# A long convolution's complex product finished on VectorE, with one inverse table and one matmul per class instead of two

## The chip, the cores and the metric

The kernel runs on one core of one Trainium2 chip. The metric is the device time of one execution in microseconds; the median of three runs counts, and lower is better.

## The reference, cut to what matters

The kernel computes one layer of a bidirectional encoder over two sequences, one of 1024 and one of 512 tokens, in fp32. Half of the mixer's width, 512 channels, goes through two gated long convolutions one after the other, each done with Fourier transforms:

```
def long_conv(z, ks, d):
    zf = jnp.fft.rfft(z, n=2 * L, axis=1)
    return jnp.fft.irfft(zf * ks[None], n=2 * L, axis=1)[:, :L] + d * z

z = x1.astype(F32) * long_conv(v.astype(F32), kspec[:, 0], bias[0])
return x2.astype(F32) * long_conv(z, kspec[:, 1], bias[1])
```

The change concerns `zf * ks`, a product of complex numbers element by element, and the first step of `irfft` behind it. The other half of the width is an mLSTM with four heads of 128 channels. Ahead of both stands an input projection, and behind them an output projection and a gated MLP.

## The kernel before

The kernel has three stages that follow one another: projections, filters and gates; then `long_convolutions_and_heads`; then the output projection and the MLP. The change lies in the second, which in the profile runs from about 766 to 1150 us.

**Tiles.** The 512 channels are worked on in two halves of HC = 256. A stream is a sequence with one half, so there are four streams: 0 and 1 for the long sequence, 2 and 3 for the short. A transform is done in two steps of matmuls. `split` (L1799) goes from tokens to classes of frequencies, and a shuffle by DMA (L1656) brings each class to its own tile. Then `forward` (L1811) transforms within a class. Two classes make a pair. The long sequence has 8 pairs and the short 4, so with two orders of convolution and two halves there are 48 pairs in all, numbered g = 0 to 47 in the order of `turns`. For each pair:

- `forward(g)` on PE: two matmuls of 128 x 128 by 128 x 256, one per class u, into `xacc[g % 2]`. Each is carried out in two passes, so the profile counts four instructions.
- `multiply(g)` on VectorE (L1983 to L1985): the spectrum in PSUM times the filter `kf` in SBUF. Partitions 0 to 63 (SUB = 64) hold real parts and 64 to 127 imaginary parts. Three products write four quarters of `prod`: real times real with imaginary times imaginary in one instruction of 128 partitions, and the two crossed products in instructions of 64 partitions, which read one half of the partitions of one operand and the other half of the other.
- `inverse(g)` on PE (L1822): for each class two matmuls, with `tab[...][1]` and `tab[...][2]`, added up in PSUM in `gacc`. They join the four quarters with their signs and transform back in one. That makes four matmuls, eight passes in the profile.
- ScalarE copies `gacc` into `classes` (L1907).

When all pairs of a stream are done, a shuffle (L1662) brings the classes back, and `join` (L1833) with `finish` on VectorE (L1993) makes tokens of them, times the gate.

**Order.** `pair_step(g)` puts `inverse(g - 2)` ahead of `forward(g)` (lag = 2). One list, `schedule`, holds the steps of convolutions and heads; the heads' steps (keys, link, attend, weight, add, square, reduce, root, unit, turn_head) are spread between them by shares written in the code. Each engine goes through the same list and carries out its part of each step, in order. In an engine's queue a step that waits holds up all behind it. `multiply(g)` stands at the place of `forward(g)`.

**Waits.** The semaphore `multiplied` counts finished products. It releases `inverse(g)`, `xacc` for `forward(g + 2)`, and the filter buffer (a ring of three) for SP's next load of `kf` (L1636). The product waits in its turn for `inverse(g - 2)` by `g_ready`, since `prod` has two buffers.

**Where lines lie.** L1883 and L1882 are the heads' attend matmuls, L1853 and L1858 keys, L1869 link and L1891 turn_head, all on PE. On VectorE L2006 weighs, L2021 to L2038 add states, L2056 to L2075 normalise heads over 512 or 1024 columns, and L2085 scales the result. L1968 is the square root on ScalarE. The inverse tables are loaded in the first stage (L841) by 12 DMAs.

## Time and profile before

| | us |
|---|---|
| median of 3 runs | 2406.47 |
| lowest, highest | 2402.73, 2407.73 |
| the profiled execution | 2401.68 |
| its span, first to last instruction | 2399.9 |
| PE busy | 2273.4 |
| VectorE busy | 1189.4 |
| ScalarE busy | 786.0 |

The profile is of one execution. Engines are called PE (TensorE matmuls), PEld (its weight loads), DVE (VectorE), ACT (ScalarE), POOL (GpSimd) and SP, the queue that issues most DMAs. PE's matmuls are pipelined, so the busy time of one overlaps that of the next, and a merged row of several tells the rate better than the duration of one. In rows of windows the engines come in the order PE, PEld, DVE, ACT, POOL. "Idle before" is the time an engine stood still ahead of an instruction, with what ended it.

### The profile page before, as it was taken

How to read it: one execution, taken by the hardware profiler on the slowest of the kernel's cores; microseconds unless marked ns; L12 is line 12 of the kernel's file. 1: busy time of each engine (PE TensorE's matmuls, PEld its weight loads, DVE VectorE, ACT ScalarE, POOL GpSimd, SP SyncE). 2: the span in 40 equal slices, each digit the busy share in tenths (PEclk: the TensorE clock that was granted, in tenths of full speed). 3: DMA queues.
4: the chain of work that ended last, by engine and by line, in shares of the span. 5: the costliest groups of instructions: out<-in, count | busy, mean ns of one | idle time of the engine just before them, and what ended most of it. 6: DMA issues, size and time to landing. Idle time of an engine off the chain costs nothing.

```text
span 2399.9 us, 26125 instructions
## 1 busy us (share of the span) xinstructions
PE 2273.4 (95%) x10340; PEld 1859.4 (77%) x10340; DVE 1189.4 (50%) x1655; ACT 786.0 (33%) x1193; POOL 146.3 (6%) x163
## 2 busy tenths in 40 slices
PE   6999999998998989778899999999999999999998
PEld 4778877886786767666688888888888887888886
DVE  6676666654832756656455333343333334324332
ACT  5432333244434434534344211222122122324221
POOL 0221122000111000100000000000000000000000
PEclk9999999999998989999999999999999999999999
DMA  4344444444556665756645111121111112535442
GB/s 144 107 142 133 125 130 138 138 161 138 190 180 175 189 189 154 236 153 185 212 133 175 50 60 53 62 79 53 59 51 62 62 53 89 183 114 174 155 148 85
DMA packets 213588, 307.22 MB, mean 128 GB/s; under 512 B 15481, under 2 KB 143865, under 8 KB 213467
## 3 DMA queue, kind: packets, MB, share of 16 engines
q1 hardware_dynamic: 200858, 256.00, 35.1%
q0 software_dynamic: 11312, 46.14, 5.2%
q10 hardware_dynamic: 1296, 3.41, 0.4%
q8 instruction: 83, 1.36, 0.2%
q14 instruction: 39, 0.31, 0.0%
HBM read 207.38 MB, written 72.16 MB: 116 GB/s over the span
## 4 chain that ended last, share of the span: by engine, by line
PE 51%; DVE 0%; ACT 0%; issue 0%; DVEq 0%; POOL 0%
PE mlp_acc L128 10%; PE mlp_acc L130 10%; PE mlp_acc L129 10%; PE mlp_dacc L128 7%; PE mlp_dacc L130 7%; PE mlp_dacc L129 7%; PE mlp_acc L2597 0%; DVE out_s_lo L2495 0%; DVE up_u L245 0%; ACT up_u L2438 0%; DVE mlp_h_lo L2517 0%; DVE out_w_lo L2490 0%; DVE down_d_lo L2539 0%; ACT out_s_hi L2413 0%; DVE up_u L249 0%
## 5 line engine op out<-in xcount | busy, mean ns | idle before, releaser
L128 PE MATMUL mlp_acc<-mlp_h_hi,up_w_hi 128*128 128x512 f32 x1056 | 411.1, 389 | 0.2 <-DVE mlp_h_lo L2517 0.2
L130 PE MATMUL mlp_acc<-mlp_h_hi,up_w_lo 128*128 128x512 f32 x1056 | 410.8, 389 | 0.0
L129 PE MATMUL mlp_acc<-mlp_h_lo,up_w_hi 128*128 128x512 f32 x1056 | 410.8, 389 | 0.0
L2522 DVE TENSOR_TENSOR up_w_lo<-up_w_raw,up_w_hi 128x1024 fp32r<-128x1024 f32 x44 | 53.8, 1225 | 388.2 <-ACT up_w_hi L2430 388.2
L128 PEld LDWEIGHTS mlp_acc<-mlp_h_hi,up_w_hi 128*128 128x128 f32 x1056 | 198.2, 188 | 41.6 <-DVE mlp_h_lo L2517 0.6
L130 PEld LDWEIGHTS mlp_acc<-mlp_h_hi,up_w_lo 128*128 128x128 f32 x1056 | 198.2, 188 | 41.2
L129 PEld LDWEIGHTS mlp_acc<-mlp_h_lo,up_w_hi 128*128 128x128 f32 x1056 | 198.2, 188 | 41.1
L128 PE MATMUL mlp_dacc<-down_d_hi,down_s_hi 128*128 128x512 f32 x528 | 206.8, 392 | 5.3 <-DVE down_d_lo L2539 5.3
L129 PE MATMUL mlp_dacc<-down_d_lo,down_s_hi 128*128 128x512 f32 x528 | 206.5, 391 | 0.0
L130 PE MATMUL mlp_dacc<-down_d_hi,down_s_lo 128*128 128x512 f32 x528 | 206.4, 391 | 0.0
L2430 ACT ACTIVATE up_w_hi<-up_w_raw 128x1024 fp32r<-128x1024 f32 x44 | 46.6, 1060 | 460.1 <-PE mlp_acc L130 460.1
L128 PE MATMUL in_acc<-in_h_hi,in_w_hi 128*128 128x512 f32 x464 | 192.9, 416 | 2.0 <-DVE in_h_lo L1168 2.0
L130 PE MATMUL in_acc<-in_h_hi,in_w_lo 128*128 128x512 f32 x464 | 182.0, 392 | 0.0
L129 PE MATMUL in_acc<-in_h_lo,in_w_hi 128*128 128x512 f32 x464 | 181.6, 391 | 0.0
L2467 ACT ACTIVATE down_s_hi<-down_s_raw 128x1024 fp32r<-128x1024 f32 (+1 forms) x72 | 70.1, 986 | 219.1 <-DMA down_s_raw<-g_scratch 144.4
L1053 ACT ACTIVATE in_w_hi<-in_w_raw 128x1024 fp32r<-128x1024 f32 x58 | 61.4, 1058 | 212.4 <-PE in_acc L130 212.4
L2545 DVE TENSOR_TENSOR down_s_lo<-down_s_raw,down_s_hi 128x1024 fp32r<-128x1024 f32 (+1 forms) x72 | 79.9, 1132 | 93.5 <-ACT down_s_hi L2467 93.5
L128 PEld LDWEIGHTS mlp_dacc<-down_d_hi,down_s_hi 128*128 128x128 f32 x528 | 99.8, 189 | 26.5 <-DVE down_d_lo L2539 5.9
L130 PEld LDWEIGHTS mlp_dacc<-down_d_hi,down_s_lo 128*128 128x128 f32 x528 | 99.8, 189 | 20.9
L129 PEld LDWEIGHTS mlp_dacc<-down_d_lo,down_s_hi 128*128 128x128 f32 x528 | 99.8, 189 | 20.8
L1174 DVE TENSOR_TENSOR in_w_lo<-in_w_raw,in_w_hi 128x1024 fp32r<-128x1024 f32 x58 | 70.9, 1223 | 73.2 <-ACT in_w_hi L1053 73.1
L128 PEld LDWEIGHTS in_acc<-in_h_hi,in_w_hi 128*128 128x128 f32 x464 | 87.5, 189 | 24.8 <-issue 6.5
(243 smaller groups left out, 3901.4 us busy)
## 6 DMA issues: line engine op xcount, KB each, us to landing
in_w_raw<-arg_w_in_t SPq DMA_DIRECT2D x58, 512.0 KB, 3.6
down_s_raw<-g_scratch SPq DMA_DIRECT2D x48, 512.0 KB, 4.7
up_w_raw<-arg_w_up_t SPq DMA_DIRECT2D x44, 512.0 KB, 3.5
g_scratch<-up_prod POOLq DMA_DIRECT2D x22, 768.0 KB, 3.5
filt_tab<-arg_fwd SPq DMA_DIRECT2D x32, 512.0 KB, 3.8
mix_classes<-mix_split SPq DMA_DIRECT2D x48, 256.0 KB, 7.9
mix_kf<-k_scratch SPq DMA_DIRECT2D x48, 256.0 KB, 3.0
mix_split<-mix_classes SPq DMA_DIRECT2D x48, 256.0 KB, 5.0
```

The costliest lines, as they stand in the source:

```text
L128: pe.matmul(out, w_hi, x_hi, start=first, stop=False)
L129: pe.matmul(out, w_hi, x_lo, start=False, stop=False)
L130: return pe.matmul(out, w_lo, x_hi, start=False, stop=last)
L1053: act.activation(w_hi[b][:, :, :], raw[b][:, :, :], ACT.Copy).then_inc(sem["w_high"], 1)
L1174: dve.tensor_tensor(w_lo[b][:, :, :], raw[b][:, :, :], w_hi[b][:, :, :].bitcast(F32), ALU.subtract).then_inc(sem["w_low"], 1)
L2430: act.activation(w_hi[i % 2][:, :, :], raw[i % 2][:, :, :], ACT.Copy).then_inc(sem["w_high"], 1)
L2467: act.activation(s_hi[b][:, kts.start:kts.stop, :], s_raw[b][:, 0:len(kts), :], ACT.Copy).then_inc(s_high[b], 1)
L2522: dve.tensor_tensor(w_lo[i % 2][:, :, :], raw[i % 2][:, :, :], w_hi[i % 2][:, :, :].bitcast(F32), ALU.subtract).then_inc(sem["w_low"], 1)
L2545: dve.tensor_tensor(s_lo[b][:, ks, :], s_raw[b][:, 0:len(kts), :], s_hi[b][:, ks, :].bitcast(F32), ALU.subtract).then_inc(s_low[b], 1)
```

## The change

The two crossed products and the two straight ones are now four instructions of 64 partitions, with the minus sign of the imaginary product in the fourth, a `scalar_tensor_tensor`. A fifth instruction adds them on 128 partitions: `whole` then holds real parts in its lower half and imaginary parts in its upper. The tables' signs are changed accordingly, the second inverse table is gone, and `inverse` has one matmul for each class. The new semaphore `crossed` counts pairs whose four products are done. It releases `xacc` and the filter buffer, and VectorE itself waits for it ahead of the sum. The wait for `g_ready` moves from ahead of the products to ahead of the sum. `prod` and `whole` have two buffers each.

```diff
--- before.py
+++ after.py
@@ -342,7 +342,7 @@
         for i in range(q):
             outer[i::q, h, i * r:(i + 1) * r] = w[:, :, h].reshape(r, r)
         outer[:, 2 + h] = outer[:, h].T
-    inner = np.zeros((P, len(tiles), 2, 3, P), np.float32)
+    inner = np.zeros((P, len(tiles), 2, 2, P), np.float32)
     m = np.arange(SUB)[:, None]
     rows = (np.arange(SUB).reshape(q, 1, nb) + SUB * np.arange(2)[:, None]).reshape(-1)
     for t, pair in enumerate(tiles):
@@ -350,9 +350,8 @@
             psi = 2 * np.pi * ((m * (2 * frequencies(s, cls)[None, :] + 1)) % (4 * n)) / (4 * n)
             co, si = np.cos(psi), np.sin(psi)
             sign = 1.0 if reflected(s, t, u) else -1.0
-            inner[:, t, u, 0] = np.block([[co, -si], [si, co]])[rows]
-            inner[:, t, u, 1] = np.block([[co.T, si.T], [-sign * co.T, -sign * si.T]])[:, rows]
-            inner[:, t, u, 2] = np.block([[-sign * si.T, sign * co.T], [-si.T, co.T]])[:, rows]
+            inner[:, t, u, 0] = np.block([[co, sign * si], [si, -sign * co]])[rows]
+            inner[:, t, u, 1] = np.block([[co.T, si.T], [sign * si.T, -sign * co.T]])[:, rows]
     return outer, inner
 
 
@@ -402,7 +401,7 @@
             f = Phase(nc, ctx, "mix", part_of=w)
             self.z = [f.sb(f"z{b}", [P, big, HC]) for b in range(2)]
             self.otab = [f.sb(f"otab{s}", [P, 4, P]) for s in range(len(SEQS))]
-            self.tab = [f.sb(f"tab{s}", [P, len(spectral_classes(s)), 2, 3, P]) for s in range(len(SEQS))]
+            self.tab = [f.sb(f"tab{s}", [P, len(spectral_classes(s)), 2, 2, P]) for s in range(len(SEQS))]
             self.cols = [f.sb(x, [P, TT, DIRS, HEADS]) for x in ("a_cols", "floor_cols", "own_cols", "past_cols")]
             self.fade = f.sb("fade", [P, DIRS, HEADS, TT])
             self.mask, self.gm = f.sb("mask", [P, DIRS, P]), f.sb("gain", [P, HEADS])
@@ -414,7 +413,7 @@
             f = Phase(nc, ctx, "out_first", part_of=w)
             f.sb("skipped", [P, big, HC])
             self.so_raw = [f.sb(f"s_raw{b}", [P, KD, P]) for b in range(2)]
-        self.size = 2 * big * HC + 2 * 4 * P + sum(len(spectral_classes(s)) for s in range(len(SEQS))) * 6 * P + 5 * TT * DIRS * HEADS + DIRS * P + HEADS
+        self.size = 2 * big * HC + 2 * 4 * P + sum(len(spectral_classes(s)) for s in range(len(SEQS))) * 4 * P + 5 * TT * DIRS * HEADS + DIRS * P + HEADS
         self.otab_loaded, self.const_loaded = w.sem("otab_loaded"), w.sem("const_loaded")
         self.z_loaded = [w.sem(f"z_loaded{st}") for st in range(4)]
         self.tab_loaded = [w.sem(f"tab_loaded{s}") for s in range(len(SEQS))]
@@ -1588,6 +1587,7 @@
             return class_slot[i][:, 2 * b0:2 * (b0 + len(blocks(st))), :]
 
         prod = [p.sb(f"prod{b}", [P, 2, 2, HC]) for b in range(2)]
+        whole = [p.sb(f"whole{b}", [P, 2, HC]) for b in range(2)]
         q, k = (p.sb(x, [P, T]) for x in ("q", "k"))
         v = p.sb("v", [P, TT, W])
 
@@ -1602,7 +1602,7 @@
         gacc = p.ps("gacc", [P, 2, HC])
         vyacc = [p.ps(f"vyacc{b}", [P, 2, HC]) for b in range(2)]
         bank = {x: p.ps(f"bank_{x}", [P, CH]) for x in "abc"}
-        names = ("v_ready v_copied x_ready multiplied g_ready g_copied "
+        names = ("v_ready v_copied x_ready crossed multiplied g_ready g_copied "
                  "y_ready z_ready transposed copied "
                  "const_set diag_ready scored k_turned k_copied exp_ready weighted linked stated attended aged combined "
                  "abs_ready norm_step squared rooted_head normed turned scaled").split()
@@ -1665,7 +1665,7 @@
 
                 def load_after(g):
                     if g + ring < len(pairs):
-                        sp.wait_ge(sem["multiplied"], g + 1)
+                        sp.wait_ge(sem["crossed"], g + 1)
                         load_k(g + ring)
 
                 def gate_after(o, st, b):
@@ -1806,7 +1806,7 @@
                         pe.wait_ge(tab_loaded[s], 16 * n_tiles[s])
                         pe.wait_ge(to_classes[st], 16 * nts[s] * (o + 1))
                     if g >= 2:
-                        pe.wait_ge(sem["multiplied"], g - 1)
+                        pe.wait_ge(sem["crossed"], g - 1)
                     for u in range(2):
                         last = pe.matmul(xacc[g % 2][:, u, :], tab[s][:, t, u, 0, :], classes(st)[:, 2 * t + u, :], start=True, stop=True)
                     last.then_inc(sem["x_ready"], 1)
@@ -1818,9 +1818,7 @@
                     if g:
                         pe.wait_ge(sem["g_copied"], g)
                     for u in range(2):
-                        for i in range(2):
-                            last = pe.matmul(gacc[:, u, :], tab[s][:, t, u, 1 + i, :], prod[g % 2][:, u, i, :],
-                                             start=i == 0, stop=i == 1)
+                        last = pe.matmul(gacc[:, u, :], tab[s][:, t, u, 1, :], whole[g % 2][:, u, :], start=True, stop=True)
                     last.then_inc(sem["g_ready"], 1)
 
                 def join_tile(o, st, b):
@@ -1977,13 +1975,15 @@
                 def multiply(g):
                     dve.wait_ge(k_loaded[g % ring], 16 * (g // ring + 1))
                     dve.wait_ge(sem["x_ready"], g + 1)
+                    x, kk, pr, to = xacc[g % 2], kf[g % ring], prod[g % 2], whole[g % 2]
+                    dve.tensor_tensor(pr[0:SUB, 0, :, :], x[0:SUB, :, :], kk[0:SUB, :, :], ALU.mult)
+                    dve.tensor_tensor(pr[0:SUB, 1, :, :], x[SUB:P, :, :], kk[SUB:P, :, :], ALU.mult)
+                    dve.tensor_tensor(pr[SUB:P, 0, :, :], x[SUB:P, :, :], kk[0:SUB, :, :], ALU.mult)
+                    dve.scalar_tensor_tensor(pr[SUB:P, 1, :, :], x[0:SUB, :, :], -1.0, kk[SUB:P, :, :], ALU.mult, ALU.mult).then_inc(sem["crossed"], 1)
                     if g >= 2:
                         dve.wait_ge(sem["g_ready"], g - 1)
-                    x, kk = xacc[g % 2], kf[g % ring]
-                    dve.tensor_tensor(prod[g % 2][:, :, 0, :], x[:, :, :], kk[:, :, :], ALU.mult)
-                    dve.tensor_tensor(prod[g % 2][0:SUB, :, 1, :], x[0:SUB, :, :], kk[SUB:P, :, :], ALU.mult)
-                    dve.tensor_tensor(prod[g % 2][SUB:P, :, 1, :], x[SUB:P, :, :], kk[0:SUB, :, :],
-                                      ALU.mult).then_inc(sem["multiplied"], 1)
+                    dve.wait_ge(sem["crossed"], g + 1)
+                    dve.tensor_tensor(to[:, :, :], pr[:, 0, :, :], pr[:, 1, :, :], ALU.add).then_inc(sem["multiplied"], 1)
 
                 def finish(o, st, b):
                     i, n = gate_of(o, st)
```

## Rows read from the trace of the kernel before

**Rows 1.** The page: busy time of each engine, and VectorE in 40 slices.

```profile
PE 2273.4 (95%) x10340; PEld 1859.4 (77%) x10340; DVE 1189.4 (50%) x1655; ACT 786.0 (33%) x1193; POOL 146.3 (6%) x163
...
DVE  6676666654832756656455333343333334324332
```

**Rows 2.** Windows of the stage: length, busy us and (instructions) per engine, PEclk, DMA, GB/s.

```profile
782.00:828.40 46.40, 41.51 (x219) 34.74 (x218) 39.84 (x71) 19.89 (x51) 2.50 (x2) 1.00 0.71 204
828.40:849.60 21.20, 21.20 (x124) 18.99 (x123) 9.38 (x28) 9.67 (x24) 0.00 (x0) 1.00 0.45 117
903.50:941.90 38.40, 36.05 (x194) 30.37 (x193) 29.62 (x56) 18.90 (x47) 2.51 (x2) 1.00 0.72 199
1089.90:1117.00 27.10, 23.97 (x126) 19.78 (x124) 24.40 (x44) 11.47 (x28) 0.00 (x0) 1.00 0.78 253
```

**Rows 3.** The tile view of mix_prod: durations in ns, minimum, median, maximum.

```profile
L1822 PE MATMUL mix_gacc<-mix_prod,mix_tab x384: 379/379/483, 784.1 to 1120.2; 128*128 128x256 f32 x192
L1983 DVE TENSOR_TENSOR mix_prod<-mix_xacc,mix_kf x48: 679/691/693, 782.0 to 1114.9; 128x512 f32<-128x512 f32 x48
L1984 DVE TENSOR_TENSOR mix_prod<-mix_xacc,mix_kf x48: 682/683/684, 782.7 to 1115.6; 64x512 f32<-64x512 f32 x48
L1985 DVE TENSOR_TENSOR mix_prod<-mix_xacc,mix_kf x48: 694/695/695, 783.4 to 1116.3; 64x512 f32<-64x512 f32 x48
```

**Rows 4.** VectorE's timeline, 798 to 803: start, us, what; x2 is two merged.

```profile
798.66 0.69 DVE L1983 TENSOR_TENSOR mix_prod<-mix_xacc,mix_kf 128x512 f32<-128x512 f32 x1
799.36 0.68 DVE L1984 TENSOR_TENSOR mix_prod<-mix_xacc,mix_kf 64x512 f32<-64x512 f32 x1
800.06 0.69 DVE L1985 TENSOR_TENSOR mix_prod<-mix_xacc,mix_kf 64x512 f32<-64x512 f32 x1
800.78 1.29 DVE L2006 TENSOR_TENSOR mix_e<-mix_bank_b,mix_e 128x512 f32<-128x512 f32 x2
801.99 0.68 DVE L1983 TENSOR_TENSOR mix_prod<-mix_xacc,mix_kf 128x512 f32<-128x512 f32 x1
```

**Rows 5.** PE's timeline of this stage, merged passes.

```profile
787.37 1.03 PE L1811 MATMUL mix_xacc<-mix_classes,mix_tab 128*128 128x256 f32 x4
788.23 1.89 PE L1822 MATMUL mix_gacc<-mix_prod,mix_tab 128*128 128x256 f32 x8
...
881.00 1.89 PE L1822 MATMUL mix_gacc<-mix_prod,mix_tab 128*128 128x256 f32 x8
...
1118.71 1.89 PE L1822 MATMUL mix_gacc<-mix_prod,mix_tab 128*128 128x256 f32 x8
```

**Rows 6.** VectorE's waits from 782 to 828.4: us in total, times, longest.

```profile
DVE mix_prod L1983 <- DMA mix_kf<-k_scratch: 1.1, 1, 1.1
...
DVE mix_e L2006 <- ACT mix_e L1936: 0.8, 1, 0.8
```

**Rows 7.** Groups by form, VectorE, 760 to 1150: busy us, mean ns, idle before.

```profile
L2085 DVE SCALAR_TENSOR_TENSOR mix_og<-mix_bank_b,mix_gain,mix_og 128x512 f32<-128x512 f32 x12 | 9.0, 750 | 7.5 <-PE mix_bank_b L1891 7.3
...
L2064 DVE TENSOR_TENSOR mix_state<-mix_state 128x512 f32<-128x512 f32 x4 | 2.8, 693 | 0.1
```

**Rows 8.** Waits of all engines, 760 to 1150.

```profile
DVE mix_prod L1983 <- DMA mix_kf<-k_scratch: 9.0, 2, 7.9
...
DVE mix_prod L1983 <- PE mix_xacc L1811: 3.3, 6, 2.5
```

**Rows 9.** Timelines of PE and VectorE around 867.

```profile
866.98 3.78 PE L1833 MATMUL mix_vyacc<-mix_split,mix_otab 128*128 128x256 f32 x8 [8.95 <-DMA mix_split<-mix_classes]
...
867.63 0.69 DVE L1983 TENSOR_TENSOR mix_prod<-mix_xacc,mix_kf 128x512 f32<-128x512 f32 x1 [7.87 <-DMA mix_kf<-k_scratch]
```

**Rows 10.** ScalarE's timeline at 972.

```profile
972.43 0.30 ACT L1968 ACTIVATE mix_rs<-mix_ss,mix_eps 128x8 f32<-128x8 f32 x1 [1.35 <-DVE mix_ss L2069]
```

**Rows 11.** Windows of 5 us, columns as in rows 2.

```profile
970.00:975.00 5.00, 2.13 (x9) 1.25 (x8) 3.79 (x4) 3.62 (x6) 0.00 (x0) 1.00 1.03 391
975.00:980.00 5.00, 4.15 (x18) 3.69 (x19) 0.19 (x1) 2.94 (x9) 2.56 (x2) 0.66 1.10 260
```

## The prediction

> **What bounds the kernel now.** I read the page first. Over the span TensorE is the busy engine, and VectorE is half idle [rows 1]; but the change touches only the stage of long convolutions and heads, so a share over the span says little. In the slice where it begins, the fourteenth, VectorE already stands at 7 tenths. The chain that ended last lies in the MLP and doesn't reach this stage, so every microsecond won or lost here moves the end by as much: the MLP waits for all of it.
>
> Then I cut the stage into stretches [rows 2]. The columns to compare are the busy times of PE and DVE against the length. There are two kinds. Stretches with pairs (782 to 828, 904 to 942, 1090 to 1117) have VectorE busy 77 to 90% of the time; stretches of joins (828 to 850) have PE busy throughout and VectorE 44%, and there no pair is worked on. The tile view gives the parts of a pair [rows 3]: eight inverse matmul passes and three VectorE products, 48 times. The timeline of VectorE shows how they queue [rows 4]: product after product without a gap, a head's operation between, and the next pair at once. PE's busy time is of overlapping passes, so I read its real rate from merged rows: 4 passes 1.03 us, 8 passes 1.89 us [rows 5], hence 0.215 us for each further pass.
>
> So in a pair stretch VectorE has no slack worth the name: 46.4 us hold 39.8 busy, most of the rest being gaps of 0.02 between operations, and the waits on others there are small, 1.1 us for a filter load, 0.8 for ScalarE [rows 2, 6]. PE is nearly as full, but about a quarter of what it does there, the inverse of each pair, waits for VectorE's product anyway.
>
> **What the change removes.** Two of four inverse matmuls of each pair, four of eight passes: 4 x 0.215 = 0.86 us of PE, 41 us over 48 pairs. The inverse tables shrink too; their loads are issued in the first stage, ahead of need, and are hidden under its matmuls: nothing gained, nothing lost.
>
> **What it adds.** VectorE's three products took 0.70 + 0.70 + 0.72 = 2.12 us from start to start [rows 4]. Halving the partitions bought nothing there: a product on 128 partitions is 691 ns and one on 64 is 683 [rows 3]. So splitting the first product in two is a full product more, not two halves. The new pair:
> - three 64-partition products at 0.70: 2.10 us;
> - the fourth is a scalar_tensor_tensor; the one on 512 columns from PSUM takes 750 ns [rows 7], so 0.77 with its gap;
> - the wait for its own engine: the sum needs the four products finished. The operations here run to their end before the next starts, so it costs a few hundredths; I put 0.01 to 0.03;
> - the sum over 128 x 512 in SBUF: 693 ns by the nearest row [rows 7]. What follows it starts sooner, though: two like operations on the same partitions take 1.29 us together, the second starting 0.61 after the first, and the product after them also follows 0.60 later [rows 4], whereas a product on other partitions than the last waits for its full end. The sum and what follows it start at partition 0 both. I take 0.61.
>
> Together 3.49 us for 2.12: 1.37 more for a pair, 65.8 us over 48. The bounds: if nothing overlaps, the sum and the wait cost 0.75, and the pair is 1.50 dearer; if all products overlap as the two like ones do, 3 x 0.61 + 0.69 + 0.61 = 3.13, 1.0 dearer. I take 1.37 since the crossing products of before did not overlap.
>
> The Trainium skill (VectorE: DVE Perf Modes, section Two Vector instructions with no wait between them) has a rule for this: an instruction is held until all before it have ended if an input or its output starts in another quadrant of partitions than the last did. By it the sum's follower is free and the crossing products are held, as taken; it would in addition free the pair's first product, which has been held behind the last pair's upper half [rows 4], about 0.1 us on some 25 pairs. By the rule the whole would come 2 to 3 us lower; without any overlap 6 us higher.
>
> **What of it is hidden.**
> - VectorE waited 9.0 us for filter loads, twice [rows 8]: 1.1 early [rows 6] and 7.87 at 867.6 [rows 9]. The latter ends with the shuffles that PE's join waits for too, queued on SP behind head loads; both ends are set by the DMA queue, not by VectorE. Three pairs stand ahead of it, whose 3 x 1.37 = 4.1 vanish in it. Hidden: 5.2.
> - It waited 3.3 us for xacc, six times [rows 8]. One, of 2.5, stands behind a join that PE bounds; the others, 0.8, vanish.
> - Waits for heads' operands off the loop: 0.8 for exponentials [rows 6], I estimate 1.2 more of that kind in the other stretches. Waits in a loop through VectorE itself (it frees a bank, PE fills it, VectorE reads it) stay.
> - PE's saving counts only where PE sets the pace: inverses that lie behind the last product of a run, among joins and heads, such as those at 881.0 and 1118.7 [rows 5]. I count nine in the PE timeline (pairs 15, 19, 27, 30, 31, 35, 38, 39 and 47): 9 x 0.86 = 7.7. The other 39, 33 us, fall into time in which PE then waits for VectorE.
>
> 65.8 - 5.2 - 0.8 - 2.0 - 7.7 = 50.1 us more.
>
> **Who is late next.** The moved wait (for the inverse two pairs before) now guards only the sum, and is long met. xacc and the filter buffer are released 2.87 us after a pair's start instead of 2.12, forward is two pairs ahead of that: no stall. PE waits at inverse for the sum, and heads' matmuls queue behind. At 972.4 even ScalarE's square root waits for VectorE's reduce [rows 10], and PE's splits wait for the copies behind it; so the three pairs ahead of it aren't hidden by PE's work there. SP's filter loads wait for the products, with ever more time.
>
> **Rivals.**
> A, slower still: PE's clock. It was at 1.00 with PE busy 2.13 us of 5, and 0.66 in the next stretch, partly at the lower level, 1.2 GHz [rows 11]. With 0.86 us less work and 1.37 more time a pair, PE is idle for more than half of each pair stretch. If the clock is at 1.2 GHz there, a pair's forward and inverse take 8 x 0.43 = 3.4 us, about VectorE's 3.5, and heads' matmuls and the joins after come on top; I estimate 20 us for some thirty pairs with heads: 50 + 20, 2476. Against it: the gaps would be short, and rows as idle as 2.13 of 5 kept 1.00. The Trainium skill (TensorE: Matmul & The Clock Gate, Part 1) says that activity releases the throttle and idleness brings it back; by it this could happen, no row shows it for gaps so short.
> B, faster: PE sets the pace in the pair stretches (it is 41.5 of 46.4 us busy in the first [rows 2]), and the added work falls into VectorE's idle time. Then 41 us are won: 2365. It decides where VectorE idles over 1.37 us a pair; in the first 13 pairs it idles 6.6 us, gaps included, 0.5 a pair [rows 2]. 0.04.
> C, no change: each run of pairs ends late on VectorE, but the join stretch behind it absorbs that, since VectorE is idle there for 11.8 of 21.2 us [rows 2]. It needs PE to go on through the joins while VectorE is late. Against it: a join's third tile takes a bank that VectorE must first empty, so PE is at most two tiles (2 us) ahead. 2406, 0.04.
> D, half hidden: products overlap (1.0 a pair, 48 - 16 = 32), or the waits that I called loops shrink: 2438. 0.12.
>
> **How the numbers follow.** My forecast, VectorE bound in the pair stretches, has 0.66; A 0.14; B and C 0.04 each; D 0.12. The profiled execution took 2401.7 us, 1.8 more than its span; the median of the runs is 2406.5, 4.8 above it. I add to both: 2451.8 for a profiled execution, 2456.6 for the median. The forecast's own range is 0.2 a pair either way: with 45 pairs that pay, 9 us, 2447 to 2466. With most of A, and D down to 32, it is 2438 to 2480. What a measurement can tell from no change is 0.2%, 5 us: faster 0.04, same 0.04, slower 0.92.
>
> **What would show it.** Right: in the profile after, VectorE's five operations of a pair start 3.4 to 3.6 us apart in the run from the first pair; 64-partition products stay at 683, the sum is near 690; that first stretch of 13 pairs is 62 us instead of 46.4; PE's inverse is 4 passes and waits for the sum; VectorE's busy time rises by some 65 us, the joins' stretch keeps 21 us. Wrong: a pair under 2.9 us, PE gap-free in pair stretches (B), or its clock under 0.9 there (A). Most likely to be mis-sized are the 7.7 us given back by PE and what is hidden ahead of 867.6.

## The result, and the profile after

The kernel after takes 2471.66 us (median, 2469.47 to 2471.85); the kernel before took 2406.26 in the runs beside it: 65 us slower. The ratio on record is 1.028, with a 95% interval of 1.0267 to 1.0294 (the two medians alone give 1.0272). The profiled execution took 2469.47 us over a span of 2467.7.

The page after, its lines that answer to [rows 1], with the slices of PE's granted clock besides:

```profile
PE 2268.4 (92%) x10148; PEld 1848.0 (75%) x10148; DVE 1249.3 (51%) x1751; ACT 786.2 (32%) x1193; POOL 147.1 (6%) x163
...
DVE  6675767645643767576546433333333333424332
...
PEclk8999999999998898888899999999999999999999
```

VectorE is busy 59.9 us more (1249.3 - 1189.4), PE 5.0 us less although 192 passes are gone. PE's clock is at 8 tenths in six slices that lie in the stage, where before it was in two that touch it. All of the loss lies in the stage: the first instruction of the MLP on VectorE starts at 1220.80 instead of 1153.18, 67.6 us later. Of these, 3.3 are there before the first pair starts (785.35 against 782.00 [rows 3]). The first stage is the same work in both kernels, and in other runs that leave it alone the first pair started anywhere from 782.3 to 786.4; I count the 3.3 as difference from execution to execution.

The tile view of mix_prod after, beside [rows 3]:

```profile
L1979 DVE TENSOR_TENSOR mix_prod<-mix_xacc,mix_kf x48: 671/676/684, 785.3 to 1180.5; 64x512 f32<-64x512 f32 x48
...
L1982 DVE SCALAR_TENSOR_TENSOR mix_prod<-mix_xacc,mix_kf x48: 683/683/685, 787.5 to 1182.6; 64x512 f32<-64x512 f32 x48
L1986 DVE TENSOR_TENSOR mix_whole<-mix_prod x48: 691/692/694, 788.2 to 1183.4; 128x512 f32<-128x512 f32 x48
...
  PE mix_xacc L1811: 13.5, 19
  DMA mix_kf<-k_scratch: 3.0, 1
...
  PEld mix_gacc L1821: 42.1, 20
  PE mix_gacc L1821: 34.0, 20
```

The durations are as forecast, but for the fourth product: 683 ns, not the 750 of [rows 7]. VectorE now waits 13.5 us for xacc, 19 times, where it waited 3.3, six times [rows 8]. That wait was forecast to vanish. The wait for filter loads fell from 9.0 to 3.0.

Windows after, columns as in [rows 2]. They cover the first 13 pairs, the joins behind them, pairs 20 to 28 (which in the kernel before began 4 us ahead of the third window), and the last eight pairs:

```profile
785.35:852.40 67.05, 42.19 (x176) 33.27 (x174) 57.16 (x97) 19.90 (x51) 3.08 (x2) 0.85 0.49 142
852.40:873.44 21.04, 20.67 (x120) 18.71 (x121) 9.32 (x28) 9.96 (x24) 0.00 (x0) 1.00 0.43 115
923.75:983.00 59.25, 40.23 (x176) 33.03 (x174) 43.92 (x79) 20.12 (x52) 2.50 (x2) 0.86 0.46 133
1145.10:1183.90 38.80, 22.96 (x98) 17.82 (x96) 34.36 (x60) 11.99 (x29) 0.00 (x0) 0.82 0.57 190
```

The first stretch went from 46.4 to 67.05 us, where 62 was forecast. The joins kept their 21 us. In these three stretches with pairs PEclk is now 0.82 to 0.86, where it was 1.00 [rows 2]. PE's instructions fell from 219 to 176 in the first stretch, but their busy time rose from 41.5 to 42.2.

VectorE's timeline at a bare pair, and at one with a head's operation behind it:

```profile
787.46 0.69 DVE L1982 SCALAR_TENSOR_TENSOR mix_prod<-mix_xacc,mix_kf 64x512 f32<-64x512 f32 x1
788.18 0.69 DVE L1986 TENSOR_TENSOR mix_whole<-mix_prod 128x512 f32<-128x512 f32 x1
788.79 0.68 DVE L1979 TENSOR_TENSOR mix_prod<-mix_xacc,mix_kf 64x512 f32<-64x512 f32 x1
...
942.10 0.68 DVE L2064 TENSOR_TENSOR mix_state<-mix_state 128x512 f32<-128x512 f32 x1
942.70 0.68 DVE L1979 TENSOR_TENSOR mix_prod<-mix_xacc,mix_kf 64x512 f32<-64x512 f32 x1
```

From pair to pair it is 3.44 us (785.35 to 788.79) to 3.50, forecast 3.49. Starts of the pairs in the two timelines, subtracted, give the step from each pair to the next. Where VectorE alone counts, the steps rose by 1.25 (2.85 to 4.10, 3.39 to 4.64) to 1.39. But some rose by 2.7 to 2.9: the steps from pair 1 (4.37 to 7.24), 9 (4.66 to 7.40), 11 (4.46 to 7.21), 24 (5.15 to 7.82), 26 (4.46 to 7.20), 27 (4.93 to 7.71) and 44 (5.14 to 7.83). These seven alone hold about 10 us beyond 1.37 each. Three more rose by over 2 us: those from pair 4 (3.58 to 5.79), 20 (12.74 to 14.86) and 32 (9.52 to 12.71), together 3.4 beyond 1.37 each. Two in which VectorE had waited for a filter or stood among joins shrank: 15 by 3.5 us and 16 by 1.6.

Step 4 has a cause of its own. VectorE's L2060, 0.69 us elsewhere, took 1.64, and GpSimd's masks ran at the same time:

```profile
808.37 1.64 DVE L2060 TENSOR_TENSOR mix_state<-mix_state 128x512 f32<-128x512 f32 x1
...
808.05 3.08 POOL L1775 TENSOR_TENSOR mix_e<-mix_e,mix_mask 128x512 f32<-128x512 f32 x2 [31.50 <-DMA mix_v<-tok_scratch]
```

In the kernel before, such an overlap fell at 1006.5 (1.75 us), in the step from pair 33.

### The profile page after: what moved, and what is told of

Read it like the earlier page. It is cut to its first block, busy times and chain, and to the rows that moved or that the text cites. A ratio compares the mean times of both kernels' runs of the same rounds, so it can differ in the third digit from the quotient of the medians.

```text
span 2467.7 us, 25883 instructions
## 1 busy us (share of the span) xinstructions
PE 2268.4 (92%) x10148; PEld 1848.0 (75%) x10148; DVE 1249.3 (51%) x1751; ACT 786.2 (32%) x1193; POOL 147.1 (6%) x163
## 4 chain that ended last, share of the span: by engine, by line
PE 49%; DVE 1%; DMA 0%; ACT 0%; issue 0%; DVEq 0%; POOL 0%; SPq 0%
PE mlp_acc L128 10%; PE mlp_acc L129 10%; PE mlp_acc L130 10%; PE mlp_dacc L128 6%; PE mlp_dacc L130 6%; PE mlp_dacc L129 6%; PE mlp_acc L2597 0%; DMA g_scratch<-up_prod 0%; DMA down_s_raw<-g_scratch 0%; DVE out_s_lo L2495 0%; DVE down_d_lo L2539 0%; DVE up_u L245 0%; DVE up_prod L2534 0%; ACT up_u L2438 0%; DVE mlp_h_lo L2517 0%
```

## The experiments

Two theories stood against each other. **V**: VectorE's longer chain is all there is, and the terms of what hides it were sized wrongly. **C** (for clock, not the rival C of the prediction): on top of the chain, PE waits long enough that its clock falls; what it does next takes longer, and VectorE then waits for it. Both have the chain in common. Runs are named by what they change; ratios are to the kernel before in the same session.

**The inverse twice.** The kernel after, each inverse matmul carried out twice, so that PE has its eight passes a pair back and VectorE's work is that of after.

```diff
-                        last = pe.matmul(gacc[:, u, :], ..., start=True, stop=True)
+                        for i in range(2):
+                            last = pe.matmul(gacc[:, u, :], ..., start=True, stop=True)
```

> The changed kernel, but each inverse matmul is carried out twice into the same bank, so that PE has as many passes a pair as before the change. The output is that of the reference. Theory V (VectorE's dearer pair alone is the loss; PE's clock costs nothing): nine inverses stand where PE sets the pace and give their 0.86 us back, 2472 + 8 = 2480. Theory C (some 50 of the 65 us are VectorE, the rest is PE's clock, which falls in the pair stretches since PE has too little to do): the added passes hold the clock up, 2462 to 2475, and the mean granted clock rises above the 0.966 of the changed kernel.

Measured: 2471.12 us, ratio 1.0282 [1.0264, 1.0299], the same as after, and within C's range; the mean granted clock rose from 0.966 to 0.972. V's rise of the total did not come. The total hides two opposite movements, which the steps show. Where PE sets the pace they grew, as V says: from pair 15 by 1.38 us, 31 by 2.22, 38 by 0.97, 39 by 0.93. But the steps from pairs 1, 11, 24, 26 and 27 shrank by 1.56, 1.36, 1.29, 1.36 and 0.75, 6.3 us in all, with more work on PE. Step 1 of the kernel after, PE's timeline and then VectorE's:

```profile
792.56 0.80 PE L1880 MATMUL mix_bank_a<-mix_state,mix_q 128*128 128x129 f32 x2 [2.50 <-DVE mix_state L2038]
...
794.01 1.91 PE L1811 MATMUL mix_xacc<-mix_classes,mix_tab 128*128 128x256 f32 x4
...
796.03 0.68 DVE L1979 TENSOR_TENSOR mix_prod<-mix_xacc,mix_kf 64x512 f32<-64x512 f32 x1 [1.25 <-PE mix_xacc L1811]
```

and with the inverse twice:

```profile
792.27 0.49 PE L1881 MATMUL mix_bank_a<-mix_state,mix_q 128*128 128x129 f32 x2 [1.64 <-DVE mix_state L2039]
...
793.04 1.03 PE L1811 MATMUL mix_xacc<-mix_classes,mix_tab 128*128 128x256 f32 x4
...
794.18 0.68 DVE L1980 TENSOR_TENSOR mix_prod<-mix_xacc,mix_kf 64x512 f32<-64x512 f32 x1 [0.20 <-PE mix_xacc L1811]
```

Read the numbers ahead of PE and in the brackets. With the inverse of four passes, PE stood idle 2.50 us and then took 1.91 us for the four passes of a forward; with eight passes it stood idle 1.64 and took 1.03, the rate of [rows 5]. 1.03 to 1.91 is close to the ratio of the two clock levels, 2.4 and 1.2 GHz, and the granted clock (the third number from the right) says it outright, first in the kernel after and then with the inverse twice:

```profile
794.00:796.00 2.00, 2.00 (x7) 1.62 (x6) 0.49 (x2) 0.19 (x1) 0.00 (x0) 0.50 0.19 66
794.00:796.00 2.00, 2.00 (x11) 1.77 (x10) 1.80 (x3) 0.17 (x1) 0.00 (x0) 1.00 0.28 98
```

VectorE waited 1.25 us in the one and 0.20 in the other. The rise that V asked for came in the paced steps (10.4 us over all steps that grew), and the slow steps that shrank made up for most of it. Steps 9 (7.40) and 44 (7.80) stayed slow: what PE is given here is not enough everywhere.

**PE's part alone.** The kernel before with one inverse matmul per class; the crossed products are computed but left out of the inverse.

```diff
-                        for i in range(2):
-                            last = pe.matmul(gacc[:, u, :], tab[s][:, t, u, 1 + i, :], prod[g % 2][:, u, i, :], ...)
+                        last = pe.matmul(gacc[:, u, :], tab[s][:, t, u, 1, :], prod[g % 2][:, u, 0, :], ...)
```

> The kernel before with the PE part of the change alone: VectorE's three products as they were, one inverse matmul a class, so the crossed quarters of the product are left out of the sum. V: VectorE sets the pace of pairs with 2.12 us as before, only the nine inverses among joins are won, 2406 - 8 = 2398. C: the same 8 us, less what a falling clock takes, 2398 to 2408, granted clock under 0.981. If PE set the pace of the pairs in the kernel before: 41 us less, 2365.

Measured: 2400.51 us, ratio 0.999 [0.9979, 1.0001]. In the steps there are gains where PE sets the pace (from pair 16, 18.27 to 15.38; from 8, 5.07 to 4.27; from 39, 52.97 to 51.36), and losses where there were none to expect: from pair 2, 3.22 to 4.73; 17, 5.64 to 7.02; 24, 5.15 to 6.45; 44, 5.14 to 6.45, together 5.5 us. The first of these is a wait for a filter load (2.64 us). In the three others the granted clock, over the step, is 0.78, 0.75 and 0.77. At the step from pair 24 PE now stands idle for longer and then runs at the lower clock. The kernel before, and then this run:

```profile
924.46 0.63 PE L1891 MATMUL mix_bank_b<-all_ident,mix_state 128*128 128x128 f32 x4 [0.76 <-DVE mix_e L2006]
924.92 1.03 PE L1811 MATMUL mix_xacc<-mix_classes,mix_tab 128*128 128x256 f32 x4
...
924.20 1.09 PE L1889 MATMUL mix_bank_b<-all_ident,mix_state 128*128 128x128 f32 x4 [2.48 <-DVE mix_e L2004]
925.08 1.91 PE L1811 MATMUL mix_xacc<-mix_classes,mix_tab 128*128 128x256 f32 x4
```

VectorE's pair is that of before, so less work on PE is enough by itself to bring such steps about. So 192 passes fewer are worth 2 us of the 7.7 forecast, and by the interval at most 5. C's range held (2398 to 2408), and V's 2398 was missed. The saving exists, and most of it is taken back elsewhere.

**Without the sum.** The kernel after, the sum left out; the inverse reads two of the four quarters, and the wait for `g_ready` is ahead of the products again.

```diff
-                    dve.wait_ge(sem["crossed"], g + 1)
-                    dve.tensor_tensor(to[:, :, :], pr[:, 0, :, :], pr[:, 1, :, :], ALU.add)...
...
-                        last = pe.matmul(gacc[:, u, :], tab[s][:, t, u, 1, :], whole[g % 2][:, u, :], ...)
+                        last = pe.matmul(gacc[:, u, :], tab[s][:, t, u, 1, :], prod[g % 2][:, 0, u, :], ...)
```

> The changed kernel without VectorE's fifth operation: the inverse reads the first two quarters of the products, the other two are left out. V: 0.61 us less for each of some 45 pairs that pay, 2472 - 27 = 2445. C: the same, and a shorter pair leaves PE less idle, so that a part of the clock's loss is gone too: 2430 to 2442, granted clock above 0.966.

Measured: 2428.08 us, ratio 1.010 [1.0083, 1.0117]. Leaving out 0.61 to 0.69 us a pair gives back 43 us, 0.9 a pair: more than the operation itself takes. The waits for xacc fall to 5.8 us. V's figure is missed and C's is passed by a little.

**Idle passes ahead of the inverse, and ahead of the first links.** Both are the kernel after. The first has two matmuls of no use (four passes) ahead of the inverse's wait for the sum.

```diff
+                    for u in range(2):
+                        pe.matmul(gacc[:, u, :], tab[s][:, t, u, 0, :], tab[s][:, t, u, 0:2, :], start=True, stop=True)
                     pe.wait_ge(sem["multiplied"], g + 1)
```

> The changed kernel with two matmuls of no use (four passes, 0.86 us) into the inverse's bank AHEAD of its wait for the sum, so that they fill time in which PE would wait. The output is that of the reference. V: hidden where PE waits, 0.86 more at nine inverses: 2472 + 8 = 2480, as the run with passes behind the wait. C: the clock is held up where it fell: 2455 to 2468, and VectorE's waits for xacc (13.5 us in the changed kernel) drop under 6.

Measured: 2472.67 us, ratio 1.0284 [1.0269, 1.03], 14.4 us of waits for xacc. The second has 16 more such passes ahead of the first link (L1867) of each head.

```diff
+                        if inverses[0]:
+                            pe.wait_ge(sem["g_copied"], inverses[0])
+                            fill(8)
                     free(before[name, ("link", j, i)])
```

> The changed kernel with idle matmuls into the inverse's bank in PE's waits: four passes ahead of each inverse's wait for the sum, and sixteen (3.4 us) ahead of the first link of each head job, where PE stood still for up to 3.5 us and then ran at half clock. Same output. C: steps from pair to pair that took 7.2 to 7.8 us in the changed kernel (from pairs 9, 11, 24, 26, 27, 44) take 5.8 to 6.5 where the clock is held, 5 to 10 us less in all, but up to 8 us more where the idle matmuls delay PE: 2463 to 2475, granted clock 0.975 or more. V: no step gets shorter, 2475 to 2490.

Measured: 2488.65 us, ratio 1.0341 [1.0325, 1.0358]. The totals did not gain, and the second cost 15 us more. C's ranges were missed in both; V's 2480 was missed in the first, and its 2475 to 2490 came in the second. The idle passes stand ahead of PE's wait, not in it, and they hold up PE's own queue. But some of the slow steps did get shorter, though PE only had more to do. In the first run those from pairs 11 and 26 fell from 7.21 and 7.20 to 5.84 and 5.85, 27 from 7.71 to 6.99 and 44 from 7.83 to 7.03; in the second 11 and 26 fell to 5.85 each and 27 to 6.32. V said of the second that no step gets shorter, so its reason failed where its total came. Steps 9 (7.40 and 7.22) and 24 (7.83 twice) stayed slow, and what was won is lost again in other steps: 11.1 and 25.8 us over all that grew. On C's sum the two runs decide nothing.

**One product more.** The kernel before with one more 64-partition product a pair, into a tile that nothing reads.

```diff
+                    dve.tensor_tensor(spare[g % 2][0:SUB, :, :], x[0:SUB, :, :], kk[SUB:P, :, :], ALU.mult)
```

> The kernel before with one more product on VectorE a pair, 64 partitions by 512 into a tile that nobody reads; PE's work is as before, the output is the reference's. It prices VectorE's time alone. V and C: 0.70 us a pair on some 42 pairs that pay, less the waits for filter loads: 24 to 30 us, ratio 1.010 to 1.0125. C: no more than that, since PE is busy enough to keep its clock: granted clock 0.976 or more. If the pair stretches had slack on VectorE: under 12 us.

Measured: 2430.95 us, ratio 1.0105 [1.0088, 1.0122]. In 37 of the 47 steps the rise is 0.5 to 0.62. None of the seven slow steps of the kernel after is slow here; three others rise by more, those from pairs 31, 36 and 41, by 1.3, 2.9 and 1.5. VectorE's timeline shows why it is 0.60 and not 0.70, as the added product is on the same partitions as the one ahead:

```profile
925.42 0.68 DVE L1985 TENSOR_TENSOR mix_prod<-mix_xacc,mix_kf 64x512 f32<-64x512 f32 x1
926.03 0.67 DVE L1986 TENSOR_TENSOR mix_spare<-mix_xacc,mix_kf 64x512 f32<-64x512 f32 x1
926.72 0.69 DVE L1987 TENSOR_TENSOR mix_prod<-mix_xacc,mix_kf 64x512 f32<-64x512 f32 x1
```

48 x 0.60 = 29 us of work, 25 of it on the path.

**Two products more.** The same with a second one into the upper half. VectorE's bare pair is then 3.33 us and PE has all its eight passes.

```diff
+                    dve.tensor_tensor(spare[g % 2][SUB:P, :, :], x[SUB:P, :, :], kk[0:SUB, :, :], ALU.mult)
```

> The kernel before with two more products of 64 partitions in each of the 48 pairs, written to tiles that nothing reads: a dose beside the run with one more (2430.95, 26 us over the kernel before for +0.60 us a pair). By the linear rule the two cost 2 x 0.60 x 48 = 58 us less the same cover, 50 to 55 us over before, 2455 to 2459. Theory C (from about +1.3 us a pair TensorE's gaps reach lengths after which the clock falls, and a second loss comes on top): more than twice the single dose, 60 us or more, 2464 to 2472, with steps of 7.2 to 7.8 us at pairs 9, 24, 26 and 27 and waits for xacc of 10 us or more, as in the kernel after, though the inverse still has its eight passes.

Measured: 2463.64 us, ratio 1.0255 [1.0237, 1.0272]. The first added product cost 25 us, the second 36. Steps from pairs 9, 24, 27 and 44 are 7.22, 7.65, 7.26 and 7.65, nearly as in the kernel after. The inverse is untouched here, so the slow steps don't come from the shorter inverse alone: VectorE's longer pair is enough for four of the seven. Those from 1, 11 and 26 stay at 5.58 to 5.67, though C had named 26. The linear rule (2455 to 2459) is out; C's 2464 to 2472, and its 10 us of waits for xacc, are missed by a hair (9.9 us).

The first 13 pairs of five kernels, from windows over each (length, PEclk), beside VectorE's bare pair:

| kernel | bare pair | 13 pairs | PEclk |
|---|---|---|---|
| before | 2.12 | 46.40 | 1.00 |
| one product more | 2.73 | 52.82 | 1.00 |
| two products more | 3.33 | 61.65 | 0.94 |
| after, inverse twice | 3.44 | 65.00 | 0.92 |
| after | 3.44 | 67.05 | 0.85 |

The first 0.6 costs 6.4 us here, the second 8.8. The last two have the same VectorE work, and differ by 2.05 us (67.05 - 65.00) and by the clock.

**Forward first.** The kernel after; on PE alone, each forward is taken out of its place behind the heads' steps and put right behind the inverse ahead of them. The same instructions, in another order on one engine.

```diff
+                for n in range(len(schedule)):
+                    if on_pe[n][0] == "forward" and pairs[on_pe[n][1]][2]:
+                        m = n
+                        while on_pe[m - 1][0] not in ("split", "forward", "inverse", "join", "turn"):
+                            m -= 1
+                        on_pe.insert(m, on_pe.pop(n))
```

> The kernel after, in TensorE's order of work alone: each forward product (L1811) is issued right behind the inverse of the pair two before, ahead of links, attends, turns and scores of heads that stood between them and that wait for VectorE or ScalarE. Nothing is computed otherwise. Theory C (the part of the loss beyond +1.37 us a pair comes where TensorE waits 2.5 to 4.5 us for VectorE in a head's step and then carries out that step and the forward queued behind it at a lower clock, 1.91 us instead of 1.03 for four passes, so that VectorE waits for xacc): the forward is done before VectorE asks for it, the 13.5 us of waits for xacc fall to under 5, the steps from pairs 9, 24, 26, 27 and 44 fall from 7.2 to 7.8 us to under 6.7, and the kernel gains 5 to 12 us, 2460 to 2466. Theory V (VectorE's longer chain alone sets the time and the waits for xacc are no part of the excess): the waits move to a head's bank on VectorE or ScalarE and the time stays within 3 us of the kernel after, 2469 to 2474.

Measured: 2459.42 us, ratio 1.0235 [1.0219, 1.025]: 11 us less than after by the ratios (1.028 - 1.0235, of 2404), 12 by the medians. Step 9 of the kernel before, on PE:

```profile
815.76 0.68 PE L1869 MATMUL mix_bank_b<-mix_v,mix_keys 128*128 128x129 f32 x4 [1.71 <-DVE mix_og L2085]
816.28 1.03 PE L1811 MATMUL mix_xacc<-mix_classes,mix_tab 128*128 128x256 f32 x4
```

of the kernel after, on PE and VectorE:

```profile
832.85 1.20 PE L1867 MATMUL mix_bank_b<-mix_v,mix_keys 128*128 128x129 f32 x4 [3.53 <-DVE mix_og L2085]
...
833.84 1.91 PE L1811 MATMUL mix_xacc<-mix_classes,mix_tab 128*128 128x256 f32 x4
834.15 0.49 DVE L2021 COPY mix_state<-mix_bank_b 128x129 f32<-128x129 f32 x2 [1.45 <-PE mix_bank_b L1867]
...
835.86 0.68 DVE L1979 TENSOR_TENSOR mix_prod<-mix_xacc,mix_kf 64x512 f32<-64x512 f32 x1 [1.22 <-PE mix_xacc L1811]
```

and with the forward first:

```profile
825.08 1.03 PE L1811 MATMUL mix_xacc<-mix_classes,mix_tab 128*128 128x256 f32 x4
...
830.01 1.20 PE L1867 MATMUL mix_bank_b<-mix_v,mix_keys 128*128 128x129 f32 x4 [3.46 <-DVE mix_og L2095]
...
831.31 0.49 DVE L2031 COPY mix_state<-mix_bank_b 128x129 f32<-128x129 f32 x2 [1.45 <-PE mix_bank_b L1867]
...
831.72 0.67 DVE L1989 TENSOR_TENSOR mix_prod<-mix_xacc,mix_kf 64x512 f32<-64x512 f32 x1
```

PE's wait is there still (3.46) and the link behind it is as slow (1.20), and VectorE waits 1.45 for it as in the kernel after. The granted clock is 0.50 in both, from 834 to 836 us there and from 830 to 832 here. What is gone is the second half: the forward was done at 826, so the product has no bracket. The seven slow steps fell to 5.40, 6.10, 5.84, 6.80, 5.57, 6.31 and 6.34, by 10.05 us in all, and the waits for xacc to 4.2 us, five times. Other steps rose by 4.4 us in all (from 45 by 1.3, from 8 by 0.9), so that from the first pair to the last the profile is 7.7 us shorter. C's marks held but for step 24, said to fall under 6.7; V expected under 3 us of gain. The same order was not tried on the kernel before with its three products, so it isn't shown that this gain belongs to the change alone.

Windows over each of the seven steps, in six kernels, settle what the totals leave open. Each cell has the length of the step in us and its granted clock; "idle passes" is the first of the two runs with such passes.

| from pair | before | after | inverse twice | idle passes | two products more | forward first |
|---|---|---|---|---|---|---|
| 1 | 4.37, 1.00 | 7.24, 0.67 | 5.68, 1.00 | 7.25, 0.67 | 5.58, 1.00 | 5.40, 1.00 |
| 9 | 4.66, 1.00 | 7.40, 0.75 | 7.40, 0.80 | 7.40, 0.74 | 7.22, 0.76 | 6.10, 0.86 |
| 11 | 4.46, 1.00 | 7.21, 0.79 | 5.85, 1.00 | 5.84, 1.00 | 5.66, 1.00 | 5.84, 1.00 |
| 24 | 5.15, 1.00 | 7.82, 0.75 | 6.53, 1.00 | 7.83, 0.78 | 7.65, 0.70 | 6.80, 0.79 |
| 26 | 4.46, 1.00 | 7.20, 0.78 | 5.84, 1.00 | 5.85, 1.00 | 5.67, 1.00 | 5.57, 0.92 |
| 27 | 4.93, 1.00 | 7.71, 0.76 | 6.96, 0.89 | 6.99, 0.88 | 7.26, 0.83 | 6.31, 0.80 |
| 44 | 5.14, 1.00 | 7.83, 0.64 | 7.80, 0.82 | 7.03, 0.91 | 7.65, 0.80 | 6.34, 0.95 |

Leave out the last column first. Wherever the clock stayed at 1.00, the step is that of before plus VectorE's added time and no more: 1.31 to 1.39 with the five operations, 1.20 or 1.21 with the two products more. Wherever it fell, the step grew by 1.9 to 2.9. In the last column steps 9, 24, 26, 27 and 44 are short although the clock fell: there the order of the queue does it alone. At 1 and 11 the clock stayed up as well, so that these two don't tell order from clock.

**The sum on GpSimd.** The kernel after, with the sum taken off VectorE.

```diff
+                    if step[0] == "forward":
...
+                        pool.wait_ge(sem["crossed"], g + 1)
+                        pool.tensor_tensor(whole[g % 2][:, :, :], prod[g % 2][:, 0, :, :], prod[g % 2][:, 1, :, :], ALU.add)...
```

> The changed kernel with the sum on GpSimd instead of VectorE; same output. VectorE's pair is then 2.80 us. If the GpSimd sum (some 1.9 us by the mask's row) fits behind it and disturbs nothing, the time is that of the run without a sum: ratio to before 1.010, 2426. If GpSimd's accesses hold VectorE's operations up, as at 1006.5 in the profile before, where one of 0.69 took 1.75: 1.015 to 1.03, and the durations of the head operations in SBUF show it.

Measured: 2461.1 us, ratio 1.023 [1.0213, 1.0248]. The sum takes GpSimd 1.27 us and VectorE is freed of it, but GpSimd's queue holds the heads' masks, which wait for loads:

```profile
794.94 1.26 POOL L1788 TENSOR_TENSOR mix_whole<-mix_prod 128x512 f32<-128x512 f32 x1 [5.39 <-DVE mix_prod L1990]
803.80 2.48 POOL L1775 TENSOR_TENSOR mix_e<-mix_e,mix_mask 128x512 f32<-128x512 f32 x2 [7.60 <-DMA mix_v<-tok_scratch]
806.24 2.48 POOL L1788 TENSOR_TENSOR mix_whole<-mix_prod 128x512 f32<-128x512 f32 x2
```

GpSimd waits 7.6 us for a load and then makes two masks, so for 10 us (796.2 to 806.2) no sum is made. PE stops at the inverse for 9.3, and VectorE waits 8.41 for xacc till 811.43. Such waits are 29.0 us, eight times, the longest 15.9. The other thing that was feared is there too, and smaller: four head operations on 128 x 512 (L2079), each begun 0.1 us behind a sum of GpSimd's, took 1718 ns on average, where they take 693 in the kernel after (L2075), 4 us in all. The profiled execution took 2453.5 us, 7.6 under the median.

**Two products, filter loaded swapped.** The kernel before, where two more DMAs a pair bring the filter with its halves exchanged, so that two products of 128 partitions do it all.

```diff
+                    for lo, hi in ((0, SUB), (SUB, P)):
+                        sp.dma_start(kf[g % ring][lo:hi, 1, :, :], k_d[s][o, t, half, SUB - lo:P - lo, :, :])...
...
-                    dve.tensor_tensor(prod[g % 2][0:SUB, :, 1, :], x[0:SUB, :, :], kk[SUB:P, :, :], ALU.mult)
-                    dve.tensor_tensor(prod[g % 2][SUB:P, :, 1, :], x[SUB:P, :, :], kk[0:SUB, :, :],
+                    dve.tensor_tensor(prod[g % 2][:, :, 1, :], x[:, :, :], kk[:, 1, :, :], ALU.mult)...
```

> The kernel before with the filter loaded a second time with its two halves of partitions swapped, so that the two crossed products become one on 128 partitions: two products a pair instead of three, PE's work unchanged, same output. V (VectorE sets the pace of pairs by the number of its operations): the pair is 1.3 to 1.4 us instead of 2.12, PE becomes the bound with 2.6 us and heads; 10 to 20 us less, 2382 to 2392. If SP's two further issues for each pair delay the shuffles: 2395 to 2410.

Measured: 2406.77 us, ratio 1.001 [0.9997, 1.0023]. The bare pair is 1.20 us instead of 2.12, and 0.9 x 48 = 43 us of VectorE's work have moved nothing: waits for kf are 35.2 us, eight times, the longest 11.6, and a load lands 4.8 us (the whole one) or 5.3 us (the halves) after its issue instead of 3.0. V's 2382 to 2392 was missed; the case of delays by the further issues (2395 to 2410) came.

**Filter in 192 rows, alone and with the forward first.** The same two products, but the first stage stores the real rows twice, so that each pair needs two whole loads instead of three.

```diff
-                    sp.dma_start(kf[g % ring][:, :, :], k_d[s][o, t, half, :, :, :])...
+                    for a in range(2):
+                        sp.dma_start(kf[g % ring][:, a, :, :], k_d[s][o, t, half, a * SUB:a * SUB + P, :, :])...
```

> The kernel before, with the filter's spectrum kept in DRAM in 192 rows (real, imaginary, real again), stored so by the first stage and loaded by two transfers of 128 rows a pair, so that each pair takes two products of 128 partitions and no third; the inverse keeps its two products per class. VectorE's pair is 1.2 to 1.4 us instead of 2.12, 0.7 to 0.9 us x 48 = 34 to 43 us less work. If the path of the pairs is VectorE's alone the time falls by 25 to 40 us, to 2365 to 2380. If TensorE (forward 0.9 to 1.0 and inverse 1.7 to 1.9 us a pair) or the landing of the loads becomes the bound, as it did when three transfers were issued for each pair, the gain is under 12 us, 2393 or more, and the trace shows waits for kf or xacc in its place. The additional stores in the first stage cost at most a few us.

> The filter in 192 rows and two products a pair, as in the run beside it, and the forward products issued ahead of the heads' steps on TensorE, as in the run beside that. If waits for xacc are what is left after the shorter pair, this run is 5 to 15 us below the one with 192 rows alone; if the filter's loads bound it, they are equal within 3 us. It is the candidate for a version below both kernels.

Measured: 2392.77 us, ratio 0.9959 [0.9946, 0.9972], the only kernel whose interval lies below the kernel before; the gain is 10 us, as said for the case that PE or the loads bound it. With the forward first 2401.59, ratio 1.0 [0.9991, 1.0009]. PE's and VectorE's timelines of the first of the two, behind the first joins:

```profile
856.13 1.97 PE L1827 MATMUL mix_gacc<-mix_prod,mix_tab 128*128 128x256 f32 x8
857.93 1.03 PE L1816 MATMUL mix_xacc<-mix_classes,mix_tab 128*128 128x256 f32 x4
858.87 1.96 PE L1827 MATMUL mix_gacc<-mix_prod,mix_tab 128*128 128x256 f32 x8
...
859.05 0.69 DVE L1988 TENSOR_TENSOR mix_prod<-mix_xacc,mix_kf 128x512 f32<-128x512 f32 x1 [0.32 <-PE mix_xacc L1816]
```

and its waits in the stage (in total, times, longest):

```profile
DVE mix_prod L1988 <- DMA mix_kf<-k_scratch: 24.3, 5, 11.3
```

Here PE is without a gap, 2.74 us a pair, and VectorE waits for it: in this stretch the bound has changed sides. Another part of the gain goes into 24.3 us of waits for the filter. With the forward first neither expectation came true, neither 5 to 15 us less nor the same. That it costs 9 us here, and gains 11 in the kernel after, I can't explain from the waits (kf 17.0, xacc 9.5); the two profiled executions differ by 3.3 us only. It stays open.

## Why the prediction was right, and where its size was off

The direction and the bound were right. The size was hit only by the wide range: 2471.66 lies outside the forecast's own 2447 to 2466, and inside 2438 to 2480 because most of rival A had been taken in. It is nearer to A's 2476 than to the forecast's 2456.6. Of the signs, the distance of pairs, the durations and the joins came as said. The first 13 pairs took 67 us, not 62, VectorE's busy time rose by 59.9, not 65, and one sign named for being wrong came too: a clock under 0.9 in the pair stretches (0.82 to 0.86). That the total lies in the range is in this respect luck.

**VectorE bounds the pair stretches: right.** The joins kept 21 us, and most steps rose by VectorE's added time. B and C of the prediction's rivals are out: the loss is neither absorbed by VectorE's idle time nor by the joins.

**1.37 us a pair: right.** Bare pairs take 3.44 to 3.50 against 3.49. Within it the fourth product was put 0.07 too dear, and the gap ahead of the sum, with the wait for the own engine in it, is up to 0.11: the sum starts 0.72 (787.46 to 788.18) to 0.79 after the fourth product, of 0.68.

**The rule on held instructions: right, and it should have been in the sum.** Row first: before, a head's operation and the pair's first product behind it were 0.72 apart (914.27 to 914.99), now they are 0.60 apart (942.10 to 942.70), and such steps rose by 1.25, not 1.37. The Trainium skill (VectorE: DVE Perf Modes, section Two Vector instructions with no wait between them) says so: an instruction is held till all before it have ended if an input or its output starts in another quadrant than in the last instruction that read or wrote that memory, with SBUF and PSUM counted apart. The trace agrees, with 0.12 us. The head's operation between them touches SBUF alone. Before, the last to read PSUM was the product that began in its upper half; now it is the fourth product, which reads from partition 0. In the sum it would have made the forecast 2 to 3 us lower, further from what came.

**Hidden, filter loads 5.2: right, within 1 us.** The waits fell by 6.0 (9.0 to 3.0).

**Hidden, waits for xacc 0.8: wrong in sign.** They rose by 10.2, to 13.5. This is where the largest part of the missing 15 us is seen. The sentence "xacc and the filter buffer are released 2.87 us after a pair's start instead of 2.12, forward is two pairs ahead of that: no stall" looked at the buffer, not at PE's queue. The forward stands behind a head's matmuls that wait for VectorE, and so it starts only when VectorE is nearly there.

**Given back by PE, 7.7: wrong net.** With PE's part alone 2 us came out. The steps that shrank did so by 10.3 us, but 5.5 us were lost in four steps that had not been slow, 4.0 of them in three where the clock fell. Doubling the inverse in the kernel after cost nothing, as slow steps shrank by 6.3 while the paced ones grew.

**Rival A, PE's clock: its mechanism happened, at a smaller price.** I gave it 0.14 and held against it that the gaps would be short. They are not: 2.50 and 3.53 us in the rows shown. It didn't slow thirty pairs by a rule of rate, as A reckoned; it struck at seven steps and in some joins.

Forecast 50, measured 65. Of the 15 between, 10 stand in the seven slow steps, and forward first, the same instructions in another order, takes them away. That the clock has a part in them is shown by the table of the seven steps, and from near by 1.91 and 1.03 us for the same four passes, at a granted clock of 0.50 and 1.00. An estimate from the rows of step 9: with the forward at 1.03 (0.88 less) and the link at its earlier 0.68 (0.52 less), the wait of 1.22 would not have been. So the loss needs two things, a queue in which the forward stands behind a waiting matmul, and a clock that has fallen by then. With the first taken away, five steps got short at a clock that had fallen. With the clock at 1.00 in the old order, steps 1, 11, 24 and 26 lost nothing beyond VectorE's time; at 9, 27 and 44 no run held it fully up. The Trainium skill (TensorE: Matmul & The Clock Gate, Part 1) says that idleness brings the throttle back; the trace agrees, with the clock at 0.85 where it was 1.00.

The clock also reaches the joins that follow on a pair. At step 32 the same four passes, behind the same short wait, in the kernel before and after:

```profile
999.12 1.13 PE L1833 MATMUL mix_vyacc<-mix_split,mix_otab 128*128 128x256 f32 x4 [0.30 <-DVE mix_z L1993]
...
1044.24 2.08 PE L1831 MATMUL mix_vyacc<-mix_split,mix_otab 128*128 128x256 f32 x4 [0.30 <-DVE mix_z L1993]
```

The clock is 1.00 from 998 to 1000 in the one and 0.50 from 1044 to 1046 in the other, behind a wait of 0.97 and of 2.36 us. Beyond 1.37 us, step 32 lost 1.8 and step 20, where the clock falls to 0.50 too, 0.75. Forward first changed neither for the better (12.73 and 15.56). Step 4 adds 0.84 by the overlap with GpSimd. These make up 3.4 of the remaining us in the profile; since steps 15 and 16 shrank by more than that, it is no exact account.

**The sum without the sum.** 43 us for one operation of 0.61 to 0.69, 25 for the first added product and 36 for the second: the cost of VectorE's work isn't linear here. The first 0.6 us a pair above the kernel before cost no more than their own 29 us; the next 0.6 cost 36. A forecast by duration times count misses that at any length of the list of terms.

## What to carry to other kernels

Splitting an elementwise operation by partitions bought no time here (683 ns for 64 partitions, 691 for 128): count instructions and columns, not partitions. Where two engines take turns, work added to the bound engine also lengthens the other's idle time, and so does work taken off the other. So look at what the granted clock of the stretch would do, and at what is queued behind the instruction that waits. And it is worth trying to take a matmul that is ready out of the queue behind one that waits for the bound engine: it gave 11 us for no instruction changed in one kernel, and cost 9 in another.

## What the runs showed of the hardware that was not expected

- Doubling the passes of a matmul 96 times (192 passes more) cost nothing in total. PE's clock was higher with them, 0.92 instead of 0.85 over the first 13 pairs. And 192 passes fewer, with VectorE's work as before, gained only 2 us.
- A scalar_tensor_tensor with a constant took 683 ns on 64 x 512 from PSUM, where one with a per-partition operand took 750 on 128 x 512 [rows 7].
- A VectorE product of 512 columns behind one on the same partitions starts 0.60 to 0.61 after it, one on other partitions 0.69 to 0.73.
- GpSimd adds 128 x 512 in SBUF in 1.27 us (median), not twice VectorE's 0.69.
- A VectorE sum with both inputs in SBUF (L2060, 128 x 512) took 1.64 us instead of 0.69 while GpSimd worked on two masks in SBUF.
